# A two-layer transformer block on one core: the prologue reads the activations first, and the adaptive-norm weights go through TensorE in column blocks

## What is computed

```
cond = silu(c)                                   # c: 1 x 1024
mod = cond @ ada_w[0] + ada_b[0]                 # ada_w[0]: 1024 x 3072
shift, scale, gate = split(mod, 3)
h = rms_norm(x, norm_g[0]) * (1 + scale) + shift # x: 512 x 1024
proj = h @ ret_w_in                              # 1024 x 6144: q, k, v, g
... retention over 4 heads ...
x = x + gate * (o @ ret_w_out)
```

## Time and profile before

| what | value |
|---|---|
| median of 3 runs | 2048.06 us (2046.82 to 2049.55) |
| the profiled execution, whole | 2050.88 us |
| its span in the trace | 2048.8 us |
| granted TensorE clock, mean of the span | 0.951 of full |
| PE busy | 1895.2 us (93%) |
| DVE, ACT, POOL busy | 815.0, 459.6, 1095.4 us |
| moved by DMA | 172.72 MB, 84 GB/s in the mean |

### The profile page before, as it was taken

The page is one execution under the profiler, slowest core; times in us unless marked ns, Lnnn a source line. Parts: engine busy times, 40 slices in busy tenths (PEclk is TensorE's granted clock), DMA queues, the critical chain, the costliest instruction groups (busy, mean ns, idle before and its releaser), DMA issues.

```text
span 2048.8 us, 27217 instructions
## 1 busy us (share of the span) xinstructions
PE 1895.2 (93%) x9694; PEld 1574.0 (77%) x9694; DVE 815.0 (40%) x1413; ACT 459.6 (22%) x933; POOL 1095.4 (53%) x856
## 2 busy tenths in 40 slices
PE   3699999999799999999999899989799779999998
PEld 3588887887688888888878677877777658887886
DVE  4615143254423333332341585885333563202300
ACT  2211112010112222212220126545213322101200
POOL 2254555557454454444356458864064467767762
PEclk8699999999799999999999899989899989999999
DMA  8322222236322322222223322100021123333331
GB/s 292 123 83 67 72 77 77 82 128 205 113 84 61 90 81 81 81 67 74 73 77 92 83 66 62 52 21 21 8 89 54 37 82 96 99 92 92 93 102 41
DMA packets 276218, 172.72 MB, mean 84 GB/s; under 512 B 5760, under 2 KB 269760, under 8 KB 274112
## 3 DMA queue, kind: packets, MB, share of 16 engines
q1 hardware_dynamic: 269136, 148.92, 24.9%
q10 hardware_dynamic: 7024, 23.02, 3.2%
HBM read 169.69 MB, written 2.10 MB: 84 GB/s over the span
## 4 chain that ended last, share of the span: by engine, by line
PE 82%; DVE 12%; ACT 2%; issue 2%; DMA 1%; POOL 1%; DVEq 0%; ACTq 0%; POOLq 0%
PE acc L370 18%; PE acc L372 17%; PE acc L371 17%; PE acc L392 3%; PE st L405 3%; PE acc L393 3%; PE acc L394 3%; PE sc L1326 2%; PE ob L1272 2%; PE sc L1306 2%; DVE ada_acc L1977 2%; DVE conv_out L2100 2%; PE bc L438 2%; DVE hn L486 1%; DMA x_tok<-in_x 1%
## 5 line engine op out<-in xcount | busy, mean ns | idle before, releaser
L676 POOL TENSOR_SCALAR wh<-raw 128x1024 fp32r<-128x1024 f32 x232 | 255.0, 1099 | 784.2 <-PE acc L372 480.7
L679 POOL TENSOR_TENSOR wl<-raw,wh 128x512 fp32r<-128x512 f32 x464 | 645.8, 1412 | 19.4
L370 PE MATMUL acc<-hh,wh 128*128 128x512 f32 x1120 | 460.4, 411 | 42.3 <-DVE ang L1906 13.9
L372 PE MATMUL acc<-hh,wl 128*128 128x512 f32 x1120 | 446.2, 398 | 0.0
L371 PE MATMUL acc<-hl,wh 128*128 128x512 f32 x1120 | 445.1, 397 | 0.0
L370 PEld LDWEIGHTS acc<-hh,wh 128*128 128x128 f32 x1120 | 216.1, 193 | 95.7 <-issue 42.8
L372 PEld LDWEIGHTS acc<-hh,wl 128*128 128x128 f32 x1120 | 215.6, 192 | 47.2
L371 PEld LDWEIGHTS acc<-hl,wh 128*128 128x128 f32 x1120 | 217.1, 194 | 45.0 <-issue 2.2
L370 PE MATMUL acc<-Yh,wh 128*128 128x512 f32 x512 | 204.3, 399 | 5.5 <-DVE xT L555 5.5
L371 PE MATMUL acc<-Yl,wh 128*128 128x512 f32 x512 | 203.6, 398 | 0.0
L372 PE MATMUL acc<-Yh,wl 128*128 128x512 f32 x512 | 203.3, 397 | 0.0
(11 more groups left out here) (386 smaller groups left out, 2693.7 us busy)
## 6 DMA issues: line engine op xcount, KB each, us to landing
raw<-in_att_w_in SPq DMA_DIRECT2D x64, 512.0 KB, 4.0
raw<-in_mlp_w SPq DMA_DIRECT2D x64, 512.0 KB, 4.0
raw<-in_ret_w_in SPq DMA_DIRECT2D x48, 512.0 KB, 3.8
ada_w<-in_ada_w ACTq DMA_DIRECT2D x8, 1536.0 KB, 8.2
raw<-in_w_in SPq DMA_DIRECT2D x23, 512.0 KB, 3.7
ada_w<-in_ada_w SPq DMA_DIRECT2D x8, 1024.0 KB, 16.5
raw<-in_ret_w_out SPq DMA_DIRECT2D x16, 512.0 KB, 4.0
raw<-in_att_w_out SPq DMA_DIRECT2D x16, 512.0 KB, 3.9
```

The source lines that it names most:

```text
L370: e.matmul(bank[:, :], wh[:, s, k, :], rhs_high(k), start=(start and k == 0), stop=False)
L372: last = e.matmul(bank[:, :], wl[:, s, k, :], rhs_high(k), start=False, stop=(stop and k == k1 - 1))
L676: e.tensor_scalar(wh[:, s, :, :], raw[:, s, :, :], 1.0, 1.0, ALU.mult, ALU.mult).then_inc(high_done, 1)
L679: low = e.tensor_tensor(wl[:, s, k0:k0 + KT // 2, :], raw[:, s, k0:k0 + KT // 2, :], wh[:, s, k0:k0 + KT // 2, :].bitcast(F32), ALU.subtract)
```

## The change

**Activations first.** x is loaded by SP ahead of all weights, as four loads of 512 KB (`x_in[t]`). PE transposes one tile of 128 positions at a time. ACT squares `x_tok[:, t, :]` with a running sum (`accum_out`) and copies out the transposes; the matmuls that summed the squares are gone.

**Adaptive weights in column blocks.** `ada_w0` is now four blocks of 512 columns, 2 MB each, in four loads with rows of 2 KB: scale, first and second half, then shift, first and second half (`ADA_PART`). A block is multiplied on PE by 8 float32 matmuls with `cond[:, 0, k]`, broadcast to 128 columns, as the stationary side, so every partition holds all 512 sums. DVE multiplies the bank with the identity, reduces each group of 128 (the diagonal), adds the bias. `ada_sum` on `ada_w0` and its 16 one-column matmuls are gone.

**First two units interleaved.** `pair` takes units 0 and 1 (in every head) together, tile by tile: (0,0) (0,1) (1,0) (0,2) (1,1) ... (0,7) (1,6) (1,7), each with its three products.

**Order and counting.** The angles and their two Sin on ACT come ahead of the blocks. The sums for the gate follow on a semaphore of their own (`VG`). `ada_g0` is loaded when PE has done block 1, behind the weights of units 2 and 3, and units 4 and 5 are loaded behind it.

```diff
+            for t in range(NT):
+                e.dma_start(x_tok[:, t, :], ins["x"][0, t * P:(t + 1) * P, :]).then_inc(x_in[t], 16)
...
+            load_ada0(0)
+            load_ada0(1)
...
-            load_ret(0, range(4))
-            load_ret(0, range(4, 6))
-            e.wait_ge(*V.at("ada0sum"))
+            load_ret(0, range(2))
+            load_ada0(2)
+            load_ada0(3)
+            load_ret(0, range(2, 4))
+            e.wait_ge(*PE.at("ada1"))
...
+            for t in range(NT):
+                e.wait_ge(x_in[t], 16)
+                if t > 0:
+                    e.wait_ge(*AC.at(f"n0ss{t - 1}"))
+                e.activation(sq[:, :, :].rearrange("p a n -> p (a n)"), x_tok[:, t, :], ACT.Square,
+                             accum_out=tc[:, t, 0:1]).then_inc(*AC.done(f"n0ss{t}"))
+                x_out(t, 0)
+                x_out(t, 1)
...
+            def ada_part(n):
+                if n >= 2:
+                    e.wait_ge(*V.at(f"mod0{n - 2}"))
+                for k in range(KT):
+                    if k % 2 == 0:
+                        e.wait_ge(ada_in[n][k // 2], 16)
+                    last = e.matmul(sc[n % 2][:, :], cond[:, 0, k:k + 1].to_broadcast([P, P]), ada_w0[n][:, k, :],
+                                    start=(k == 0), stop=(k == KT - 1))
+                last.then_inc(*PE.done(f"ada{n}"))
+
+            e.wait_ge(*V.at("cond"))
+            ada_part(0)
             norm_spread(e, "n0")
-            e.wait_ge(*V.at("ada0sum"))
-            ada_columns(e, ada_acc0, 0, 16, "ada0cols")
+            for n in range(1, 4):
+                ada_part(n)
...
-                for j in range(4):
-                    e.wait_ge(*(V.at(f"r_g{j + 2}", i - 1) if j < 2 else AC.at(f"r_qk{j - 2}", i)))
-                    feat(e, acc[j % 2], c + j, U["ret"] + j, inputs="n0" if j == 0 else None)
+                pair(e, c, U["ret"], "n0", [V.at(f"r_g{j + 2}", i - 1) for j in range(2)])
+                for j in range(2, 4):
+                    e.wait_ge(*AC.at(f"r_qk{j - 2}", i))
+                    feat(e, acc[j % 2], c + j, U["ret"] + j)
...
+            def ada_part(n):
+                part, k0 = ADA_PART[n]
+                e.wait_ge(*PE.at(f"ada{n}"))
+                picked = dg[:, :].rearrange("p (k n) -> p k n", k=4)
+                step(e, e.tensor_tensor(picked, sc[n % 2][:, :].rearrange("p (k n) -> p k n", k=4),
+                                        ident.unsqueeze(1).to_broadcast([P, 4, P]), ALU.mult), V)
+                m = mod[:, 0, part, k0:k0 + 4]
+                step(e, e.tensor_reduce(m, picked, AX.X, ALU.add), V)
+                step(e, e.tensor_tensor(m, m, sm("ada_b0", part * KT + k0, 4), ALU.add), V, f"mod0{n}")
...
+            ada_part(0)
+            e.wait_ge(*AC.at(f"x{2 * NT - 1}"))
+            e.wait_ge(*PE.at("n0bc"))
+            for k in range(4):
+                normed(k)
+            ada_part(1)
+            for k in range(4, KT):
+                normed(k)
+            ada_part(2)
+            for k in range(4):
+                low(k)
+            ada_part(3)
+            for k in range(4, KT):
+                low(k)
             for k in range(KT):
-                e.wait_ge(ada_in[k], 32)
-                ada_sum(e, ada_accg[:, :], ada_g0[:, k, :], k, "ada0gsum" if k == KT - 1 else None)
+                e.wait_ge(gate_in[k], 16)
+                gate_sum(e, k)
```

More of the change, by code:

```diff
@@ L211, in build @@
         W = 64 * KB
-        ada_w0 = at("ada_w0", [P, KT, 2 * D], 0)
+        ada_w0 = [at(f"ada_w0{n}", [P, KT, S], n * 16 * KB) for n in range(4)]
+        ADA_PART = [(1, 0), (1, 4), (0, 0), (0, 4)]
         ada_g0 = at("ada_g0", [P, KT, D], 0)
         x_tok = at("x_tok", [P, NT, D], W)
-        ada_acc0 = at("ada_acc0", [P, 2 * D], W + 16 * KB)
         ada_accg = at("ada_accg", [P, D], W + 39 * KB)
@@ L378, in feat, with pair @@
             product(e, bank, u, c, lambda k: hh[:, k, :], lambda k: hl[:, k, :], inputs=inputs)
+        def pair(e, u, c, inputs=None, free=None):
+            order = [(0, 0), (0, 1)]
+            for k in range(KT):
+                order += [(1, k)] + ([(0, k + 2)] if k + 2 < KT else [])
+            for b, k in order:
+                s = (c + b) % RING
+                if k == 0:
+                    e.wait_ge(split_done, u + b + 1)
+                    if free is not None:
+                        e.wait_ge(*free[b])
+                if b == 0 and inputs is not None:
+                    e.wait_ge(*V.at(f"{inputs}h{k}"))
+                e.matmul(acc[b][:, :], wh[:, s, k, :], hh[:, k, :], start=(k == 0), stop=False)
+                e.matmul(acc[b][:, :], wh[:, s, k, :], hl[:, k, :], start=False, stop=False)
+                last = e.matmul(acc[b][:, :], wl[:, s, k, :], hh[:, k, :], start=False, stop=(k == KT - 1))
+                if k == KT - 1:
+                    last.then_inc(unit_used, 1)
         def tok(e, u, c, tag, free, lh=hh, ll=hl, tiles=NT, between=None):
@@ L779, in _ @@
             e.activation(cos_[:, :], tmp[:, 1, :], ACT.Sin).then_inc(*AC.done("rope"))
+            e.wait_ge(*V.at("mod02"))
+            for k in range(KT):
+                if k == 4:
+                    e.wait_ge(*V.at("mod03"))
+                e.wait_ge(*V.at(f"n0t{k}"))
+                e.activation(hh[:, k, :], hn[:, k, :], ACT.Identity, bias=mod[:, 0, 0, k:k + 1]).then_inc(*AC.done(f"n0hi{k}"))
             with e.Fori(0, RH) as i:
@@ L1870, in _ @@
             count_from(e, V)
+            count_from(e, VG)
             e.memset(ones[:, :], 1.0).then_inc(*V.done("ones"))
@@ new lines, in normed, with low @@
+            def normed(k):
+                e.scalar_tensor_tensor(out=hn[:, k, :], in0=xT[:, k, :], scalar=gain[:, 0, k:k + 1], in1=bc[:, :],
+                                       op0=ALU.mult, op1=ALU.mult).then_inc(*V.done(f"n0t{k}"))
+            def low(k):
+                e.wait_ge(*AC.at(f"n0hi{k}"))
+                e.scalar_tensor_tensor(out=hl[:, k, :], in0=hn[:, k, :], scalar=mod[:, 0, 0, k:k + 1],
+                                       in1=hh[:, k, :].bitcast(F32), op0=ALU.add, op1=ALU.subtract)\
+                 .then_inc(*V.done(f"n0h{k}"))
```

79 lines of the change are left out of this document (41 added, 38 removed).

## The result

| | before | after |
|---|---|---|
| median of 4 runs | 2048.64 us (2046.82 to 2049.55) | 1998.95 us (1998.41 to 2000.1) |
| ratio after to before | | 0.9759 (95%: 0.9742 to 0.9776) |
| profiled execution, span | 2050.88, 2048.8 us | 1999.29, 1997.5 us |
| granted TensorE clock, mean | 0.951 | 0.968 |
| fifth unit of the first head starts | 103.23 | 66.91 |

The direction was right, and so was the mechanism in the prologue; 13 us came from somewhere else.

The account below looks back on a forecast made before the run. PE was taken to bound the kernel (82% of the last chain). 43.5 + 0.5 + 21.8 + 0.8 put the fifth unit at 66.6 us, 36.6 less, so 2048.06 - 36.6 = 2011.5 us; range 2005.5 to 2023.

Parts of the forecast that it names:

- Start of the blocks: Prologue on PE: ACT starts at 6.5 us, 2.5 us per tile of x, last transposes end at 14.5 us.
- The blocks: Prologue on PE: 32 float32 matmuls of 512 columns take 28.0 us at full clock, four spread matmuls 1.0, ending at 43.5.
- Data keeps up: Prologue loads: 2 KB rows move at about 390 GB/s, so block 3 is in by 36 us, before PE begins it at 36.5.
- Copy waits vanish: First head: both copy waits, on the first head's count and on ACT's first copy, vanish under work.
- The fifth unit at 66.6: First head: the fifth unit starts at 66.6 us, including 0.8 of the 0 to 2 us tile 4 or splits may cost.
- Later heads gain nothing from `pair`: Heads after the first: no gain, with both units' weights ready and unit 2's copy done within the pair's last 1.4 us.
- full after 24 idle microseconds: Clock before the transposes: read as full after PE's idle start, as evidence against applying the rule that transposes don't count.
- the low clock at the blocks' start: Rival: transposes with gaps let the clock fall, 6 us at half rate as blocks start; +3, 2014.5 us; chance 0.22.
- the longer low clock: Rival: float32 blocks don't lift the clock for 20 us, +10, 2021.5, or for all, +28, 2039.5; chance 0.12.
- late data: Rival: 2 KB rows move at only 290 GB/s, PE loses 2 to 4 us; 2014.5 us; chance 0.08.
- a held count: Rival: another first-head count holds PE or ACT until the gate's sums end near 62; +9, 2020.5 us; chance 0.04.
- the slow outcome: Rival: block matmuls' stationary loads aren't hidden and the clock is low throughout; 2053.5 us, slower than before; chance 0.02.

Follow-up runs that it names:

- e5: The changed kernel with the gate's sums counted on DVE's common semaphore again, as before the change; 2008.54 us, ratio 0.9822 to the kernel before.
- e1: The kernel before with only `pair` added (units 0 and 1 interleaved in every head); 2032.64 us, ratio 0.9933 to the kernel before.
- e3: The kernel before, without `pair`, POOL's split of unit 4 in heads 1 to 3 held until unit 1 is done; 2032.75 us, ratio 0.9938.
- e2: The changed kernel without `pair`, units 0 and 1 one after the other again; 2010.65 us, ratio 0.9826 to the kernel before.
- e4: The changed kernel with `pair`, plus an extra POOL split into unread buffers at the three head boundaries; 2010.18 us, ratio 0.9825 to the kernel before.
- e8: The changed kernel without `pair`, POOL's split of unit 4 in heads 1 to 3 held until unit 1 is done; 2002.07 us, ratio 0.9788.

## Why the prediction was wrong, point by point

- **Start of the blocks, 14.5: measured 14.82.** The parts were off in both directions. The transposes waited for `const` until 7.64 and ran at half clock at first, with ACT standing 2.18 us behind them, where I had nothing late; but ACT starts at 5.4 and not at 6.5, and a tile of x costs it 2.0 us from square to square (10.14, 12.13, 14.13) and not 2.5. That the sum came within 0.3 is partly luck.
- **The blocks, 28.0 + 1.0 at full clock: measured 28.0 in all,** from 14.82 to the first projection at 42.82, without a gap between blocks. The 0.5 for entering the loop was not needed.
- **Data keeps up at an estimated 390 GB/s: measured 388 to 391** in the stretches above. The trace's 290 for 512-byte rows and 412 for 4 KB rows were the right ends to draw the line between. The rule that the prediction cites from the Trainium skill's page "DMA: Bandwidth & Descriptors", Specifications, line rate from 512 B on, did not hold for these loads: the measurements decide.
- **Copy waits vanish, and there is none ahead of unit 2: right.** e5 shows that the separate semaphore carries it.
- **The fifth unit at 66.6, with 0.8 of stall: measured 66.91, with 1.73.** The stall is POOL's: raw unit 4 landed at 55.38 and not at 53, and the splits were slowed by DVE's sums, as the earlier trace rows had shown. That the two ends agree so well is partly luck: the first projection came 1.2 us sooner than 43.5 + 0.5, and units 0 to 3 without the stall took 22.4 us and not 21.8.
- **"Later heads gain nothing from `pair`: both units' weights lie ready, and unit 2's copy is done within the pair's last 1.4 us." This is the step that failed,** and with it "what follows is dense". It looked at PE's inputs (the weights) and at its next bank, but not at what `pair` releases. A unit's end frees a slot for POOL; interleaving units 0 and 1 moves the end of unit 0, and with it POOL's next split, some 4 us later (from the half of the pair's 10.9 us to 1.4 us before their end), and so off DVE's last steps, on which ACT's copy hangs. The last part of the sentence was wrong for its own reason too: the copy of unit 0 waits for DVE's end of the head before, as the three 2.6 us waits before show. They stood in the 11.4 us of PE's waits for `ret_q`, of which I had used only the prologue's 3.57. Price: 10.3 us in the traces (3 x 3.43, of each 1.85 waiting and the rest, by subtraction, the clock behind it). Over the heads it is 10.4 in e1, 10.1 in e3, 8.7 in e2 and 9.1 in e4; the last two have a fall of the clock at two of the three boundaries only. The whole times give 8.8 to 13.3.
- **The remaining 4.8 us of the span** are clock falls that vary from execution to execution, three in the profiled execution before that the one after does not have. Between the medians 3.1 us of it are left: 36.3 + 10.3 = 46.6 stands against 49.7 measured. Between the medians measured again nothing is left (2047.4 - 2001.41 = 46.0). The range held 2 to 3 us for how runs differ; what it lacked are the 10.3.
- **The clock, "full after 24 idle microseconds": a misreading.** The 1.00 printed there is the lack of a record; by the transposes' own pace PE began at half clock, at 24 us before and at 7.64 after. The blocks did start at full clock, as the sum has it, but because the transposes had lifted it by 13.01, not because it had been full all along: that term came out right by luck. By the transposes' own pace the slow start cost them an estimated 2 us (19 of them, 0.21 instead of 0.11 us apart). The rule cited from the Trainium skill ("TensorE: Matmul & The Clock Gate", Part 4), that transposes don't count, is not borne out either: the clock rose during them in every trace.
- **The rivals:** the low clock at the blocks' start was given 0.22 and shows in one of nine executions; the longer low clock, late data, a held count and the slow outcome didn't come. The prediction's own range had no case with a gain behind the fifth unit, and this, more than any size, is why the time fell out of it.

## What to carry to other kernels

When an edit makes PE finish units in another order, follow each of its releases as well as its inputs: which engine starts what at the new time, and beside what. A stall at PE that is named after ACT may have its cause two engines back, in two-input DVE steps that run against POOL; comparing the same steps' durations with and without POOL busy shows it, and a hold of one unit on POOL is a far cheaper edit than the interleaving. And list every wait of the engine that bounds the kernel, in the whole loop, before saying that a part of the loop has nothing to gain.

## What the hardware showed that I had not expected

**POOL and DVE slow each other by what they read.** The boundary's DVE steps by form: line, operation, count, busy, mean ns. Before:

```profile
L1953 DVE TENSOR_TENSOR Yl<-ret_k,Yh 128x512 f32 x8 | 10.4, 1335 | 0.0
...
L1959 DVE SCALAR_TENSOR_TENSOR ret_k<-ret_k,small,bc 128x512 f32<-128x512 f32 x8 | 5.9, 735 | 0.0
```

After:

```profile
L2045 DVE TENSOR_TENSOR Yl<-ret_k,Yh 128x512 f32 x8 | 7.4, 931 | 1.0 <-ACT Yh L860 1.0
L2051 DVE SCALAR_TENSOR_TENSOR ret_k<-ret_k,small,bc 128x512 f32<-128x512 f32 x8 | 5.9, 739 | 0.0
```

The step with both inputs in SBUF loses 0.4 us in the mean; the one whose second input is the bank `bc` loses nothing (at 173.10, beside POOL's `tensor_tensor` of 172.72, it took 0.73). And where before's first `Yl` was slow (171.64, 1.53 long), it ended 0.54 us behind POOL's instruction (171.44 + 1.19), about the length of its own work. The Trainium skill, page "SBUF — State Buffer", section "Who interferes with whom", says just this: a DVE instruction with two SBUF inputs contends with a GpSimd instruction that reads SBUF, one with at most one such input (outside DVE's two-port modes) does not, and the loser blocks fully. These rows agree with it. Applied to the earlier trace rows and to the heads' boundary it could have pointed at the missing 10 us before the run.

**The clock's falls are partly chance.** From the same 2.00 us wait on PE took 24.41 or 25.95 us to the next start, 96 matmuls later, in executions of the same kernel; behind the 0.78 us waits at the changed kernel's boundaries there was no fall, and behind 2.63 us there was one at each boundary of the kernel before, but at two of e2's three only (87.09 us from its first boundary to the second, 88.68 from the second to the third), and in e4 none behind 3.02 us and one behind each 2.69. In e8 there was one more in its first head, after waits of 1.57 and 0.73 us. What decides it is open.

**PE starts at half clock, and a printed 1.00 can hide it.** In every trace here the first transposes run at the pace of the lower level, whether they start at 7 or at 24 us, and the step up comes while PE does only transposes. Before the first record of the clock, go by the length of the same matmul early and late.
